# Second block's mixing loop: scores two heads ahead, output products inside the last turns, three weight remainders on GpSimd

## The chip, the cores and the metric

One core of one Trainium2 chip. The metric is device time in microseconds (us) of one execution. Below, PE is TensorE, DVE is VectorE, ACT is ScalarE, POOL is GpSimd and SP the engine whose queue issues the weight loads.

## What is computed

Two transformer blocks of two layers each on 256 tokens of width 1024, in float32. The change touches the mixing stage of the second block, once in each of its two layers:

```python
proj = h @ w_in[layer]
(qa, ka, va, qb, kb, vb, qi, ki, wi, qc, kc, vc) = jnp.split(proj, split_points, axis=-1)
...
oa = moba_attention(qa, ka, heads(va, N_HEADS_A))                    # 4 heads, softmax
ob = dsa_attention(qb, kb, heads(vb, N_HEADS_B), qi, ki, wi)         # 4 heads, top-64 keys, softmax
oc = stick_breaking_attention(heads(qc, N_HEADS_C), ...)             # 8 heads
...
o = jnp.concatenate([oa, ob, oc], axis=2)
o = (_rms(o).reshape(B, S, D_MIX) * out_g[layer]).astype(x.dtype)    # rms per head of 64
x = x + g2 * (o @ w_out[layer])
h = modulate(rmsnorm(x, norm_g[layer, 2]), sh3, sc3)
x = x + 0.5 * g3 * swiglu_2(h, ffn_w1[layer, 1], ffn_w3[layer, 1], ffn_w2[layer, 1])
```

Stick-breaking takes, with z the scaled scores, A = exp(z - sum over later keys of softplus(z)), where softplus(z) = max(z, 0) + log(1 + exp(-|z|)).

## The kernel before

**Weights.** All weights come as a stream of tiles of 128 x 2048 (1 MB) through a ring of four buffers (`stream_in`, L371): the load of tile p waits until PE has finished tile p - 4 (`tile_done`). Each product is made in three passes for precision (`triple`, L332): ACT rounds the tile to its high part (`high`, L320, semaphore `w_hi_ready`), DVE writes the remainder over the tile in the ring (`low`, L327, `w_lo_ready`), and PE multiplies high by high, high by low and low by high. The activations are split likewise into `h_hi` and `h_lo`.

**Tiles of the mixing stage.** Tile n is weight tile Z_QI + n. Tiles 0 to 14 project (`tile(n)`: 48 products of 256 columns each), 15 to 18 are the four tiles of `w_out` (named Z_O to Z_O + 3), and behind them the feed-forward begins (Z_O + 4 onward). ACT copies each projection out of PSUM (`evac(n)`, L2439 for n > 10) and then splits a tile three ahead. Tiles 13 and 14 share PSUM bank 3, so that tile 14 waits for `evac(13)`. While tiles 9 to 12 run, DVE selects the top 64 keys and makes remainders in between; the last, that of tile 14, ends just before the loop.

**The loop.** Eight turns handle one softmax head and one stick-breaking head each, and up to four more drain. The order of each engine is written out by hand; engines meet by semaphores only. On PE a head n needs `scores_sticks(n)` (L2307 to L2311), `flip(n)` (L2318: transposes of the probabilities), `sums(n)` (L2327 to L2331: the sum over later keys as products) and two `weigh` (L2347 to L2351: products with the values); for each pair of heads `turn_back` (L2360) transposes the normed output. DVE has `soften` (L2683: scale, mask; L2686, L2687: maxima), `stick` (L2692), `stick_log` (L2700: both inputs in SBUF), `stick_arg` (L2708), and for each pair `pair_stat` (L2713), `pair_scaled` (L535 to L537, L2725), `pair_low` (L2734). ACT has `exps` (L2481, L2483), `softplus` (L2492 to L2494), `flipped` (L2500: copies what flip wrote, `pt_ready`), `sticked` (L2504), and for each pair `pair_sq` (L2509), `pair_rstd` (L2514, L2515), `pair_high` (L2521). Heads n and n + 1 use different PSUM banks (4 and 5; 0 and 1 for the sticks), `sums` has bank 2, `flip` bank 6.

One turn of PE before the change:

```python
if i + 1 < HEADS_2: scores_sticks(i + 1)
if i in (0, 2): tile(13 + i // 2)
flip(i - 1); sums(i - 1)
if i >= 5 and i % 2 == 1: turn_back((i - 5) // 2)
weigh(n, 0, ...); weigh(n, 1, ...)      # n = i - 2
```

**Behind the loop.** `out_part(c, half, b, pair)` makes six products of 512 columns (two k, three passes) for token half b and column half c. 24 products per tile of `w_out`: first Z_O and Z_O + 1 for both token halves, turn_back 3 between them, then the other two tiles, with token half 0 first (`out_done`), token half 1 last. ACT splits Z_O + 3 and then Z_O + 4 (`next_high`), DVE makes their remainders; that of Z_O + 4 stands in `shift_dve` ahead of the gate (L724, L726: output times gate row), residual (L731), norm and shift. POOL, once the loop's last `weigh` is done, issues the loads of three rows of the modulation, 512 KB each as broadcast (L2802), and in the first layer that of `c_row` (L966).

## Time and profile before

| | us |
|---|---|
| median of 3 runs (lowest, highest) | 2841.31 (2838.57, 2844.32) |
| the profiled execution's own time | 2839.58 |
| its span, first to last instruction | 2837.5 |
| PE busy | 2766.8 (98%) |
| DVE busy | 1951.3 (69%) |
| ACT busy | 1366.8 (48%) |
| POOL busy | 228.7 (8%) |

The mixing loop runs twice: from about 2009 to 2060 and from about 2565 to 2618 us of the span. A busy PE is not one at its peak, since the ends of matmuls are modelled; start to start distances tell the pace. "Idle before" in a timeline row is the time in which the engine did nothing, and behind the arrow stands what ended it.

### The profile page before, as it was taken

To read this page: it belongs to the slowest core of one execution; us is meant where nothing else is said; L and a number is where in the kernel's file an instruction comes from. 1 tells how busy PE (TensorE), PEld (TensorE's weight loads), DVE (VectorE), ACT (ScalarE), POOL (GpSimd) and SP (SyncE) were. 2 spreads that over 40 slices of the span, in tenths; PEclk is the share of its full clock that TensorE was granted. 3 is DMA by queue.
4 is the path that set the end of the run, shared out by engine and by line. 5 is a ranking of instruction groups with operands and counts; after the bars stand their busy time and mean duration, and the time that the engine had idled before them with its cause. 6 is when DMAs were issued, how large, how long until landed. Compare 5 with 4: busy or idle time off the path is not lost.

```text
span 2837.5 us, 37822 instructions
## 1 busy us (share of the span) xinstructions
PE 2766.8 (98%) x16120; PEld 2426.8 (86%) x16120; DVE 1951.3 (69%) x2187; ACT 1366.8 (48%) x1562; POOL 228.7 (8%) x201
## 2 busy tenths in 40 slices
PE   8999999999999999999999999999899999999999
PEld 6889999998888889999998887878878878788787
DVE  6668876655666678877655667677876676677644
ACT  5444545455444445545454444444644444446433
POOL 0000420000000000520000000003000000030000
PEclk9999999999999999999999999999999999998999
DMA  8655433445766655333446666653266676442454
GB/s 306 257 220 183 149 125 136 164 164 210 263 261 248 248 208 189 138 136 132 171 165 228 257 255 243 260 218 134 90 244 251 239 274 253 177 150 95 176 189 148
DMA packets 82038, 564.42 MB, mean 199 GB/s; under 512 B 9072, under 2 KB 10576, under 8 KB 15952
## 3 DMA queue, kind: packets, MB, share of 16 engines
q1 hardware_dynamic: 66272, 465.47, 44.8%
q0 software_dynamic: 15600, 96.55, 9.0%
q8 instruction: 127, 2.08, 0.3%
q14 instruction: 39, 0.32, 0.0%
HBM read 560.86 MB, written 1.12 MB: 198 GB/s over the span
## 4 chain that ended last, share of the span: by engine, by line
PE 78%; DVE 13%; ACT 4%; POOL 2%; issue 2%; DMA 1%; SPq 0%; POOLq 0%; ACTq 0%; DVEq 0%
PE ps L332 71%; DVE ring_lo L327 4%; ACT w_hi L320 2%; POOL qk L2038 1%; PE ps L899 1%; POOL rope_a L2034 1%; DVE a_hg L1806 1%; DMA rows<-mod_rows 1%; DMA ring<-stream 1%; DVE e L1786 1%; DVE e L1785 1%; PE ps L1287 1%; DVE h_lo L576 0%; PE ps L1416 0%; PE ps L1442 0%
## 5 line engine op out<-in xcount | busy, mean ns | idle before, releaser
L327 DVE TENSOR_TENSOR ring_lo<-ring,w_hi 128x2048 fp32r<-128x2048 f32 x422 | 973.8, 2310 | 484.0 <-ACT w_hi L320 473.0
L320 ACT ACTIVATE w_hi<-ring 128x2048 fp32r<-128x2048 f32 x422 | 806.4, 1911 | 318.6 <-PE ps L332 188.0
L332 PE MATMUL ps<-w_hi,h_hi 128*128 128x512 f32 (+1 forms) x1920 | 728.9, 380 | 18.1 <-DVE ring_lo L327 9.0
L332 PE MATMUL ps<-w_hi,h_lo 128*128 128x512 f32 (+1 forms) x1920 | 717.0, 373 | 0.0
L332 PE MATMUL ps<-ring_lo,h_hi 128*128 128x512 f32 (+1 forms) x1920 | 716.3, 373 | 0.0
L332 PEld LDWEIGHTS ps<-w_hi,h_hi 128*128 128x128 f32 x1920 | 363.7, 189 | 85.6 <-DVE ring_lo L327 11.3
L332 PE MATMUL ps<-h_hi,w_hi 128*128 128x256 f32 x1488 | 431.6, 290 | 1.4 <-DVE h_lo L576 1.3
L332 PE MATMUL ps<-h_lo,w_hi 128*128 128x256 f32 x1488 | 423.0, 284 | 0.0
L332 PE MATMUL ps<-h_hi,ring_lo 128*128 128x256 f32 x1488 | 423.0, 284 | 0.0
L332 PEld LDWEIGHTS ps<-w_hi,h_lo 128*128 128x128 f32 x1920 | 363.2, 189 | 64.7
L332 PEld LDWEIGHTS ps<-ring_lo,h_hi 128*128 128x128 f32 x1920 | 363.8, 189 | 60.7 <-issue 1.0
L332 PEld LDWEIGHTS ps<-h_hi,w_hi 128*128 128x128 f32 x1488 | 287.6, 193 | 7.2 <-issue 5.9
L332 PEld LDWEIGHTS ps<-h_lo,w_hi 128*128 128x128 f32 x1488 | 287.8, 193 | 2.8 <-issue 2.4
L332 PEld LDWEIGHTS ps<-h_hi,ring_lo 128*128 128x128 f32 x1488 | 287.5, 193 | 0.0
L332 PE MATMUL ps<-w_hi,g_hi 128*128 128x512 f32 x576 | 224.6, 390 | 1.6 <-DVE g_lo L1083 1.6
L332 PE MATMUL ps<-w_hi,g_lo 128*128 128x512 f32 x576 | 224.1, 389 | 0.0
L332 PE MATMUL ps<-ring_lo,g_hi 128*128 128x512 f32 x576 | 224.1, 389 | 0.0
L993 DVE CUSTOM_DVE_ANT_0 e<-e,val 128x1024 f32<-128x1024 f32 x154 | 181.6, 1220 | 5.7 <-ACT val L1000 5.7
L1041 ACT ACTIVATE g_hi<-ps 128x512 fp32r<-128x512 f32 x80 | 47.7, 596 | 223.2 <-PE ps L899 223.2
L981 POOL DMA_DIRECT2D e<-ada x77 | 40.7, 529 | 1121.3 <-DVE mod_sum L993 822.9
L332 PEld LDWEIGHTS ps<-w_hi,g_hi 128*128 128x128 f32 x576 | 108.1, 188 | 24.7 <-DVE g_lo L1083 2.4
L332 PEld LDWEIGHTS ps<-w_hi,g_lo 128*128 128x128 f32 x576 | 108.1, 188 | 22.5
(359 smaller groups left out, 3437.4 us busy)
## 6 DMA issues: line engine op xcount, KB each, us to landing
ring<-stream SPq DMA_DIRECT2D x438, 1024.0 KB, 4.8
e<-ada POOLq DMA_DIRECT2D x77, 1024.0 KB, 6.2
rows<-mod_rows POOLq DMA_DIRECT2D x18, 512.0 KB, 5.7
rows<-gain_rows POOLq DMA_DIRECT2D x8, 512.0 KB, 4.8
val<-c_row POOLq DMA_DIRECT2D x4, 512.0 KB, 5.3
x<-x_in SPq DMA_DIRECT2D x4, 256.0 KB, 6.7
mem<-mem_t SPq DMA_DIRECT2D x1, 1024.0 KB, 16.2
out_t<-x SPq DMA_DIRECT2D x4, 256.0 KB, 2.1
```

What stands on the lines that cost most here:

```text
L320: nc.scalar.activation(hi_of(p), ring[:, p % RING, :], ACT.Copy).then_inc(S.w_hi_ready, 1)
L327: nc.vector.tensor_tensor(lo_of(p), ring[:, p % RING, :], hi_of(p).bitcast(F32), ALU.subtract).then_inc(S.w_lo_ready, 1)
L332: mm = nc.tensor.matmul(out, a, b, start=start and n == 0, stop=stop and n == 2, skip_group_check=group)
L899: mm = nc.tensor.transpose(ps[:, bank, a * T + b * P:a * T + (b + 1) * P], g_f[:, i % 2, b, a * P:(a + 1) * P], ident)
L981: pool.dma_start(e_buf[(i + 1) % 2][:].rearrange("p k t -> p (k t)"), ada[l * 2 * PER_FFN + first + i]).then_inc(ada_loaded[(i + done) % 2 ...
L993: ins = nc.vector.tensor_tensor_reduce(part, part, silu_c, 1.0, 0.0, ALU.mult, ALU.add, mod_sum[:, at + n:at + n + 1])
L1041: nc.scalar.activation(g_hi[:, g_slot(i - 1), :], ps[:, 2 * ((i - 1) % 2), :], ACT.Copy).then_inc(S.ghi_ready, 1)
L1287: mm = nc.tensor.matmul(ps[:, 4 + 2 * g + j // 2, at:at + n], sta[:, hd, t * P:(t + 1) * P], right, start=True, stop=True)
L1785: nc.vector.tensor_tensor(lo, lo, halves(hk, half)[0], ALU.mult)
L1786: nc.vector.tensor_tensor(hi_, hi_, halves(hq, half)[1], ALU.mult).then_inc(S.e_ready, 1)
L1806: ins = nc.vector.copy_predicated(dst.rearrange("p a (g two c) -> p a g two c", two=2, c=c)[:, :, :, 1, :], upper(mask, c).unsqueeze(1).br ...
L2034: nc.gpsimd.tensor_tensor(rope_a[:], part, cos1[:].unsqueeze(1).broadcast_to([P, 2, T]), ALU.mult).then_inc(S.pool_chain, 1)
```

## The change

On PE: tile 13 runs before the loop; scores 0 and 1 come ahead of it, tile 14 in turn 0, and each turn i then makes scores i + 2 between flip and sums (scores 4 at the end of turn 2). In turns 8 and 9 `out_ahead` puts the products of Z_O and Z_O + 1 for token half 0, 12 for each pair of heads; behind the loop token half 1 has 24 left, and turn_back 3 follows these. On ACT: `evac(13)` and `evac(14)` end turns 0 and 1, and the split of Z_O + 3 goes ahead of `pair_high` in the last turn. On DVE: the remainders of Z_O to Z_O + 2 are gone, `stick_log` comes before `stick_arg`, `pair_scaled` after both, and the remainder of Z_O + 3 ahead of the last `pair_low`. POOL makes the three remainders, four pieces of 128 x 512 each.

```diff
@@ -2285,7 +2285,7 @@
                                               fq[r, 4, 0:P * (qt + 1)], start=True, stop=True)
                         if i == len(even) - 1:
                             mm.then_inc(S.logit_done, 1)
-            for n in range(9, 13):
+            for n in range(9, 14):
                 tile(n)
 
             def scores_sticks(n):
@@ -2361,24 +2361,6 @@
                                                  o_tok[:, j, at:at + P], ident)
                 mm.then_inc(S.o_turned, 1)
 
-            scores_sticks(0)
-            for i in range(HEADS_2 + 2):
-                if i + 1 < HEADS_2:
-                    scores_sticks(i + 1)
-                if i in (0, 2):
-                    tile(13 + i // 2)
-                if 0 <= i - 1 < HEADS_2:
-                    flip(i - 1)
-                    sums(i - 1)
-                if i >= 5 and i % 2 == 1:
-                    turn_back((i - 5) // 2)
-                n = i - 2
-                if 0 <= n < HEADS_2:
-                    weigh(n, 0, n, pt2[:, n % 2, :], S.pt_ready, S.pv_done)
-                    weigh(n, 1, stick_head(n), st[:, 6 + n % 2, :], S.a_ready, S.o_done)
-            pe.wait_ge(S.arg_ready, nth(S.arg_ready, HEADS_2))
-            pe.wait_ge(S.scores_read, nth(S.scores_read, HEADS_2))
-
             def out_part(c, half, b, pair):
 
                 at = 2 * half + pair
@@ -2389,15 +2371,43 @@
                                 half == 1 and pair == 1 and i == 1)
                 return mm
 
-            pe.wait_ge(S.o_ready, nth(S.o_ready, 2))
+            def out_ahead(pair):
+
+                pe.wait_ge(S.o_ready, nth(S.o_ready, pair + 1))
+                if pair == 0:
+                    pe.wait_ge(S.zm_ready, nth(S.zm_ready, HEADS_2))
+                for c in range(2):
+                    pe.wait_ge(S.w_lo_ready, Z_O + c + 1)
+                    out_part(c, 0, 0, pair)
+
+            scores_sticks(0)
+            scores_sticks(1)
+            for i in range(HEADS_2 + 2):
+                n = i - 2
+                if i == 0:
+                    tile(14)
+                if 0 <= i - 1 < HEADS_2:
+                    flip(i - 1)
+                if i + 2 < HEADS_2 and i != 2:
+                    scores_sticks(i + 2)
+                if n >= HEADS_2 - 2:
+                    out_ahead(n - HEADS_2 + 2)
+                if 0 <= i - 1 < HEADS_2:
+                    sums(i - 1)
+                if 0 <= n < HEADS_2:
+                    weigh(n, 0, n, pt2[:, n % 2, :], S.pt_ready, S.pv_done)
+                if i >= 5 and i % 2 == 1:
+                    turn_back((i - 5) // 2)
+                if 0 <= n < HEADS_2:
+                    weigh(n, 1, stick_head(n), st[:, 6 + n % 2, :], S.a_ready, S.o_done)
+                if i == 2:
+                    scores_sticks(4)
+            pe.wait_ge(S.arg_ready, nth(S.arg_ready, HEADS_2))
             for c in range(2):
-                pe.wait_ge(S.w_lo_ready, Z_O + c + 1)
                 for pair in range(2):
-                    for b in range(2):
-                        mm = out_part(c, 0, b, pair)
+                    mm = out_part(c, 0, 1, pair)
                 mm.then_inc(S.tile_done, 1)
-                if c == 0:
-                    turn_back(3)
+            turn_back(3)
             pe.wait_ge(S.o_ready, nth(S.o_ready, 3))
             for c in range(2):
                 pe.wait_ge(S.w_lo_ready, Z_O + 2 + c + 1)
@@ -2524,27 +2534,24 @@
 
             nc.scalar.preload_act_table_set("natural_log_exp_and_others")
             for i in range(HEADS_2 + 4):
-                if 0 <= i - 2 < HEADS_2 and i != 3:
+                if 0 <= i - 2 < HEADS_2:
                     flipped(i - 2)
                 if i >= 5 and i % 2 == 1:
                     pair_rstd((i - 5) // 2)
                 if i < HEADS_2:
                     exps(i)
-                if i == 3:
-                    softplus(i)
-                    evac(14)
-                    flipped(i - 2)
                 if 0 <= i - 2 < HEADS_2:
                     sticked(i - 2)
+                if i == HEADS_2 + 3:
+                    next_high(act, Z_O)
                 if i >= 4 and i % 2 == 0:
                     pair_sq((i - 4) // 2)
                 if i >= 5 and i % 2 == 1:
                     pair_high((i - 5) // 2)
-                if i < HEADS_2 and i != 3:
+                if i < HEADS_2:
                     softplus(i)
-                if i == 1:
-                    evac(13)
-            next_high(act, Z_O)
+                if i < 2:
+                    evac(13 + i)
             next_high(act, Z_O + 1)
             shift_act(act, 2, Z_O + 2)
             ffn_act(act, FFN_D, 1, None, row=2 + DEPTH if l < DEPTH - 1 else None)
@@ -2743,20 +2750,17 @@
                 if i < HEADS_2:
                     soften(i)
                     stick(i)
-                if i == 3:
-                    low(dve, Z_V + 6 + HIGHS)
+                if 0 <= i - 1 < HEADS_2:
+                    stick_log(i - 1)
+                if 0 <= i - 2 < HEADS_2:
+                    stick_arg(i - 2)
                 if i >= 5 and i % 2 == 1:
                     pair_scaled((i - 5) // 2)
-                if 0 <= i - 2 < HEADS_2:
-                    stick_arg(i - 2)
-                if 0 <= i - 1 < HEADS_2:
-                    stick_log(i - 1)
-                if i == 1:
-                    low(dve, Z_V + 5 + HIGHS)
-                if i == 5:
-                    low(dve, Z_V + 7 + HIGHS)
                 if i >= 4 and i % 2 == 0:
                     pair_stat((i - 4) // 2)
+                if i == HEADS_2 + 3:
+                    dve.wait_ge(S.w_lo_ready, Z_O + HIGHS)
+                    low(dve, Z_O + HIGHS)
                 if i >= 5 and i % 2 == 1:
                     pair_low((i - 5) // 2)
 
@@ -2771,7 +2775,6 @@
                     dve.wait_ge(S.ada_done, nth(S.ada_done, PER_FFN))
                     vectors_two(chain, l + 1)
 
-            low(dve, Z_O + HIGHS)
             shift_dve(dve, chain, 2, Z_O + 2, row_count + 6, 0, z_ready)
             ffn_dve(dve, l, DEPTH, FFN_D, 1, False, products=l < DEPTH - 1, between=ahead)
             ready = ffn_ready(dve, FFN_D, 1)
@@ -2833,6 +2836,21 @@
                 nc.gpsimd.tensor_tensor(part, rope_a[0:r, 0:n, :], rope_b[0:r, 0:n, :],
                                         ALU.add).then_inc(S.rope_done, 1)
             send_mods(pool, l, 5, 9, sent + 2, sent + 2)
+            Z_O = tiles_2(l)[3]
+
+            def low_part(j, c):
+                p, at = Z_O + j, slice(c * 512, (c + 1) * 512)
+                if c == 0:
+                    pool.wait_ge(S.w_lo_ready, p)
+                    pool.wait_ge(S.w_hi_ready, p + 1)
+                ins = nc.gpsimd.tensor_tensor(lo_of(p)[:, at], ring[:, p % RING, at], hi_of(p)[:, at].bitcast(F32),
+                                              ALU.subtract)
+                if c == 3:
+                    ins.then_inc(S.w_lo_ready, 1)
+
+            for j in range(HIGHS):
+                for c in range(4):
+                    low_part(j, c)
             pool.wait_ge(S.o_done, nth(S.o_done, HEADS_2))
             row(ROW_GATE, l, 5)
             row(ROW_SHIFT, l, 6)
```

ACT at the loop's start, before: head 0's exponentials (L2481, L2483) and softplus (L2492 to L2494), those of head 1, and only then the copy of tile 13 (L2439) and the split of a weight tile (L320).

```order
L2481 ACTIVATE prob_20_66,e1<-prob_20_66,small 128x128
L2483 ACTIVATE prob_20_66,e1<-prob_20_66,small 128x256
L2492 ACTIVATE a_hg<-a_hg 128x384
L2493 ACTIVATE a_hg<-a_hg 128x384
L2494 ACTIVATE a_hg<-a_hg,one 128x384
L2481 ACTIVATE prob_21_67,e1<-prob_21_67,small 128x128
L2483 ACTIVATE prob_21_67,e1<-prob_21_67,small 128x256
L2492 ACTIVATE a_hg<-a_hg 128x384
L2493 ACTIVATE a_hg<-a_hg 128x384
L2494 ACTIVATE a_hg<-a_hg,one 128x384
L2439 ACTIVATE qk<-ps 128x512
L320 ACTIVATE w_hi<-ring 128x2048
```

The same place in the changed kernel, from head 0's second exponential on; its lines are 10 higher here (L2449 is the copy).

```order
L2493 ACTIVATE prob_20_66,e1<-prob_20_66,small 128x256
L2502 ACTIVATE a_hg<-a_hg 128x384
L2503 ACTIVATE a_hg<-a_hg 128x384
L2504 ACTIVATE a_hg<-a_hg,one 128x384
L2449 ACTIVATE qk<-ps 128x512
L320 ACTIVATE w_hi<-ring 128x2048
L2491 ACTIVATE prob_21_67,e1<-prob_21_67,small 128x128
L2493 ACTIVATE prob_21_67,e1<-prob_21_67,small 128x256
L2502 ACTIVATE a_hg<-a_hg 128x384
L2503 ACTIVATE a_hg<-a_hg 128x384
L2504 ACTIVATE a_hg<-a_hg,one 128x384
L2449 ACTIVATE qk<-ps 128x512
```

One copy and split stand after head 0 and one after head 1; before, tile 14's copy came in turn 3.

DVE behind the last pair, before: the refinement and scaling of pair 3 (L535 to L2725), its low part (L2734), and two remainders (Z_O + 3, Z_O + 4) ahead of the gate (L724).

```order
L537 SCALAR_TENSOR_TENSOR e<-e 128x8
L2725 TENSOR_TENSOR hk<-ps,e 128x512
L2734 SCALAR_TENSOR_TENSOR h_lo<-ps,v_now,h_hi 128x256 x2
L327 TENSOR_TENSOR ring_lo<-ring,w_hi 128x2048 x2
L724 TENSOR_TENSOR e<-ps,rows 128x512
L726 TENSOR_TENSOR e<-ps,rows 128x512
```

The same in the changed kernel (L2732 is the scaling, L2741 the low part).

```order
L537 SCALAR_TENSOR_TENSOR e<-e 128x8
L2732 TENSOR_TENSOR hk<-ps,e 128x512
L327 TENSOR_TENSOR ring_lo<-ring,w_hi 128x2048
L2741 SCALAR_TENSOR_TENSOR h_lo<-ps,v_now,h_hi 128x256 x2
L327 TENSOR_TENSOR ring_lo<-ring,w_hi 128x2048
L724 TENSOR_TENSOR e<-ps,rows 128x512
```

The remainder of Z_O + 3 has moved ahead of the low part; that of Z_O + 4 still stands between the low part and the gate.

## Rows read from the trace of the kernel before

**Rows 1.** The page, part 1: busy time and share of the span.

```profile
PE 2766.8 (98%) x16120; PEld 2426.8 (86%) x16120; DVE 1951.3 (69%) x2187; ACT 1366.8 (48%) x1562; POOL 228.7 (8%) x201
```

**Rows 2.** Timeline of PE: start us, us, engine, line, operation, idle before and releaser.

```profile
2009.04 0.34 PE L2307 MATMUL ps<-qk 64*128 64x128 f32 x1 [0.78 <-ACT qk L2439]
...
2019.69 0.38 PE L332 MATMUL ps<-h_hi,w_hi 128*128 128x256 f32 x1
...
2025.54 0.49 PE L2318 MATMUL ps<-con_sb,prob 128*128 128x128 f32 x3
...
2055.12 0.52 PE L2318 MATMUL ps<-con_sb,prob 128*128 128x128 f32 x3 [1.26 <-ACT prob_t L2500]
...
2058.74 0.66 PE L2360 MATMUL ps<-con_sb,hk 128*128 128x128 f32 x4 [0.93 <-DVE hk L2725]
...
2060.49 0.48 PE L332 MATMUL ps<-w_hi,h_hi 128*128 128x512 f32 x1
...
2575.39 0.38 PE L332 MATMUL ps<-h_hi,w_hi 128*128 128x256 f32 x1
```

**Rows 3.** Windows: stretch, its us, busy us of PE, PEld, DVE, ACT, POOL, clock.

```profile
2029.50:2054.50 25.00, 19.22 (x137) 16.66 (x137) 18.11 (x44) 17.52 (x48) 0.00 (x0) 0.93 0.02 6
```

**Rows 4.** Chain of waits in time, behind the first loop: start us, us, what.

```profile
2060.68 5.56 PE ps L332 x24
...
2066.25 6.76 DMA ring<-stream
...
2075.13 2.29 DVE ring_lo L327
2077.43 0.60 DVE e L724
```

**Rows 5.** DMA issues from 2626 to 2627: KB each, us to landing.

```profile
ring<-stream SPq DMA_DIRECT2D x1, 1024.0 KB, 4.7
```

**Rows 6.** Chain of waits behind the second loop.

```profile
2618.53 7.70 PE ps L332 x24
...
2637.62 0.70 DVE e L726
```

**Rows 7.** Timeline of DVE: the first softening.

```profile
2012.81 0.56 DVE L2683 SCALAR_TENSOR_TENSOR prob<-ps,con_sb 128x384 f32<-128x384 f32 x1
```

**Rows 8.** Timeline of ACT: exponentials of heads 0 and 1, copy of flip 6.

```profile
2014.05 0.40 ACT L2481 ACTIVATE prob<-prob,small 128x128 f32<-128x128 f32 x1 [2.05 <-DVE small L2687]
...
2016.56 0.39 ACT L2481 ACTIVATE prob<-prob,small 128x128 f32<-128x128 f32 x1
...
2054.51 0.47 ACT L2500 ACTIVATE prob_t<-ps 128x384 f32<-128x384 f32 x1
```

**Rows 9.** Timelines of POOL and of DVE in the rotary stage.

```profile
1957.48 1.28 POOL L2828 TENSOR_TENSOR rope_a<-qk,con_sb 128x512 f32<-128x512 f32 x1 [12.28 <-DVE qk L2608]
1959.45 3.20 POOL L2833 TENSOR_TENSOR qk<-rope_a,rope_b 128x512 f32<-128x512 f32 x1 [0.69 <-DVE rope_b L2617]
...
1979.73 3.26 POOL L2828 TENSOR_TENSOR rope_a<-qk,con_sb 128x512 f32<-128x512 f32 x1 [2.87 <-DVE qk L2608]
...
1959.23 2.28 DVE L327 TENSOR_TENSOR ring_lo<-ring,w_hi 128x2048 fp32r<-128x2048 f32 x1
1961.43 1.78 DVE L535 SCALAR_TENSOR_TENSOR e<-e 128x512 f32<-128x512 f32 x1
1963.24 0.69 DVE L536 TENSOR_TENSOR e<-e 128x512 f32<-128x512 f32 x1
...
1981.78 0.68 DVE L2617 TENSOR_TENSOR rope_b<-ps,con_sb 128x512 f32<-128x512 f32 x1
```

**Rows 10.** Windows around the norm ahead of the mixing stage.

```profile
1909.50:1913.00 3.50, 0.59 (x5) 0.35 (x3) 3.24 (x6) 1.93 (x5) 0.00 (x0) 1.00 0.94 384
...
1918.30:1923.27 4.97, 4.93 (x23) 4.96 (x24) 4.91 (x3) 1.31 (x2) 0.00 (x0) 0.50 0.02 3
```

**Rows 11.** Timeline of POOL: the row loads behind the first loop.

```profile
2061.23 1.57 POOL L2802 DMA_DIRECT2D rows<-mod_rows  x3 [74.12 <-PE ps L2351]
```

## The prediction

> **What bounds the kernel now.** I read first the page's share of each engine: PE is busy 98% of the span [rows 1], so a change pays only where PE waits, runs at half clock or is itself on the chain. Then the timeline of the mixing loop of the second block's first layer ("layer A"; the second, "layer B", runs the same 555.70 us later, by the starts of its tile 14 [rows 2]). There PE waits for ACT's copy of the transposed probabilities before flip 7 at 2055.12 and for DVE before turn_back 2 at 2058.74 [rows 2]. Third, the engines over the loop's middle: of 25.00 us PE is busy 19.22, DVE 18.11, ACT 17.52 [rows 3]. Nobody is full: the loop is a ring of waits through the three. Last, the chain behind the loop. In layer A it leaves PE after 24 output products (5.56 us) and goes through the load of the feed-forward's first weight tile (6.76), its split on ACT and its remainder on DVE (2.29); only then does DVE gate the first half row, at 2077.4 [rows 4]. In layer B, where that load takes 4.7 us [rows 5], the chain stays on PE's products, up to DVE's second gate product at 2637.62 [rows 6]. That one follows the first by 0.6 where nothing waits [rows 4], so B's gate counts as 2637.0, or 2081.3 on A's scale. This instant, the gate, sets the time of a layer.
>
> **Start of the loop.** Tile 13 now stands ahead of scores 0. Tile 12 ends at 2008.26 (scores 0 at 2009.04 after 0.78 of idle [rows 2]); a tile takes 5.85 (2019.69 to 2025.54 [rows 2]), so scores 0 starts near 2014.05. A head's scores take 0.9 there, so DVE's first softening starts at 2014.95, where it was 2012.81 [rows 7]: 2.1 us later. ACT begins 1.24 after a softening (2012.81 to 2014.05) and takes 2.51 for a head's exponentials and softplus (2014.05 to 2016.56 [rows 8]), so to 2018.7. Only then comes the copy of tile 13 (0.6), for which tile 14 waits, as both lie in PSUM bank 3. PE stands from about 2015.8 to 2019.3; tile 14 runs to 2025.2, against 2025.54. ACT copies tile 14 and splits the next weight tile (1.9) and is free at 2027.6. Before, it got there at 2029.5, 1.9 later, but with two more heads' exponentials and softplus (5.0), one copy (0.47 [rows 8]) and one stick exponential (0.5) done: 6.1 us of work more.
>
> **Middle of the loop.** From there to the copy that frees flip 7 (2054.51 [rows 8]) ACT did 17.5 us of work and waited 7.5 [rows 3]. Now it has 17.5 + 6.1 to do. Its waits shrink, since scores come two turns ahead, but they don't go: `pair_high` stands ahead of softplus in each odd turn and still needs the scaling on DVE and turn_back on PE. Following the queues turn by turn with these durations, I get two such waits of about 2 us and small ones, 4.6 in all. 2027.6 + 23.6 + 4.6 = 2055.8, so flip 7 starts at 2056.5, after 0.5 for the copy and a restart: 1.4 later than before. The three remainders that leave DVE's loop (2.29 each) earn nothing by this: DVE has 7 us to spare in the stretch [rows 3], and at 2038 the remainder lay beside turn_back and `pair_high`.
>
> **Tail of the loop.** From flip 7 to the first output product took 5.37 us (2055.12 to 2060.49 [rows 2]), some 1.2 of it the stand before turn_back 2 (0.93 as idle, the rest its restart); 4.15 of work stay. Two groups of 12 products go in, at 5.56/24 = 0.232 each, 5.6. PE leaves the loop at T = 2056.5 + 9.7 = 2066.2. Before, it left at 2060.49 and had those 24 products yet to do: 2066.05. So the filling alone gains nothing: the largest stand of the last turns is before flip 7, and the first group is queued behind it.
>
> **GpSimd's remainders.** One 128x512 product takes it 1.28 us alone and 3.20 beside a DVE remainder; the DVE instruction behind took 1.78 where the next took 0.69; a DVE product of PSUM and one SBUF operand beside a busy GpSimd took 0.68, no more [rows 9]. So in the loop only `stick_log`, with both inputs in SBUF, can be hit. The twelve products end near 2033 (the third tile starts when ACT is done, at 2027.6), or at 12 x 3.26 = 39 us after 2012.8, 2052, at worst, before their first use at 2056.9: no wait of PE. But stick_log 1 and 2 fall at 2027.7 and 2030.9, and ACT waits for what follows them. Bounds 0 and 2.6 (two whole products); by the row's excess, 1.78 - 0.69 = 1.09 each, 2.2; I take 1.5, as they need not meet exactly. The Trainium skill (SBUF — State Buffer, Who interferes with whom) says that a DVE instruction with two SBUF inputs and a GpSimd one that reads SBUF lock each other out for the whole instruction; by that rule, with which the row agrees, the term would be up to 2.6.
>
> **Clock.** In the trace 3.5 us with 0.59 of PE work were followed by the half clock, 1.2 GHz, with 23 products in 4.93 us, 0.214 each [rows 10]. The new stand before tile 14 is as long. At half clock its 48 products, 5.85/48 = 0.122 each, cost up to 48 x 0.092 = 4.4 more; nothing if the clock holds. I take 1.5: only the products until the clock is back count. T = 2069.2.
>
> **After the loop.** The load on layer A's chain starts with the last product of the first output tile. That was 5.76 after T (2066.25 less 2060.49); of 24 products 12 remain, so it is now T + 2.95. The row loads on GpSimd's queue are issued 0.75 after T (2061.23 [rows 11]); the weight load came 5.0 after them and will come 2.2 after. It competes with them from its start. Least, 6.76 as before; most, a landing 11.8 after the row loads' issue as before (2061.23 to 2073.01), T + 12.5, if only the bytes count. I take T + 10.7. From landing to gate are 4.4 (2073.0 to 2077.4): T + 15.1 = 2084.3, against 2077.4, **6.9 later**. Layer B has one row load fewer: landing T + 10, gate T + 14.4 = 2083.6, against 2081.3, **2.3 later**. What is behind the gate (norm, transposes, feed-forward) moves as a whole. 9.2 in all.
>
> **Sum.** The profiled execution took 2839.58 (span 2837.5); plus 9.2 is 2848.8. The median of the runs is 2841.31; by it, 2850.5. I put 2849.5. With the open terms at their lower ends (no lock-out, clock held, load 6.76 in A and 4.7 in B) A is 2.9 later and B 3.1 earlier: 2839.4. At the upper (2.6, 4.4, landings T + 12.5 and T + 11.2) A is 12.7 later, B 7.5: 2859.8.
>
> **Rivals.** *No change* (0.25): the lower ends hold, 2839.4 to 2843. For it: two of the terms can be nothing. Against: the load's place next to the row loads is no chance. *Faster* (0.17), by filling: if scores two turns ahead bring flip 7 to 2050.8 instead of 2056.5, T is the 2060.5 of before with 24 products done. Then the gate is at T + 14.1 in A (2.8 earlier) and T + 12.05 in B (8.8 earlier, its half clock, 7.70 for 24 products [rows 6] where A has 5.56, gone): 2828. It gains over 0.2% from T = 2063.4 down. For it: ACT and DVE have 7 us of waits there. Against: ACT's late start, and pair_high's place in its queue. *Half clock behind the loop in both layers* (0.12): in B it cost 2.1 on 24 products and as much in the loop; 4.3 a layer on top of the forecast, 2858. *GpSimd late* (0.03): it would need over 43 us; each us beyond is one us in each layer, some 2855. My forecast has the rest, 0.43.
>
> **Numbers.** 0.2% is 5.7 us, about what a measurement of this kernel can tell. Slower by more: forecast, half clock and GpSimd, 0.58. Within: 0.25. Faster: 0.17. The range runs from 2832, part of the way into the faster case, to 2860.
>
> **What would show it.** In the changed kernel's layer A: PE idle some 3.5 us before tile 14, ended by ACT's copy; flip 7 between 2056 and 2060 with an output product right after it; turn_back 2 behind the second group with no wait; GpSimd's products 1.3 to 3.3 us each and done before 2050; one or two stick_logs of over 0.55 us; the feed-forward's first tile issued 3 us after the loop, its remainder on DVE ending after the products that the gate needs. If flip 7 comes before 2051, or the load lands within 5 us, I am wrong on the side of faster.

## The result, and the profile after

| | before | after |
|---|---|---|
| median us (lowest to highest) | 2841.28 (2838.57 to 2844.32) | 2863.98 (2862.16 to 2864.03) |
| the profiled execution | 2839.58 | 2864.03 |
| mean granted clock of PE | 0.992 | 0.983 |

The changed kernel takes 1.0082 of the time of the kernel before (95% interval 1.0066 to 1.0098), 22.7 us more. Slower was forecast, at 2849.5 us; the measured time lies outside the range of 2832 to 2860.

I compared the start of each matmul with the same matmul in the trace before. The changed kernel is already 5.0 us late at 1982 us, in code that is the same in both. It loses 11.9 us in layer A and 7.3 in layer B, 19.2 together. Of the 5.0, 2.5 and 1.1 come up at two stretches of the first block that went at 1.2 GHz here and at 2.4 GHz before, as the windows of the two traces show (stretch, its us, busy us and instructions of PE, PEld, DVE, ACT, POOL, clock, DMA share, GB/s). Kernel after:

```profile
385.60:392.40 6.80, 6.80 (x34) 6.80 (x34) 6.80 (x4) 1.91 (x1) 4.37 (x3) 0.50 0.13 54
1218.50:1225.30 6.80, 6.80 (x33) 6.80 (x33) 5.76 (x3) 5.90 (x8) 6.58 (x3) 0.50 0.05 19
```

Kernel before:

```profile
385.60:392.40 6.80, 6.80 (x60) 6.80 (x58) 6.80 (x4) 1.96 (x2) 3.80 (x2) 1.00 0.04 17
1218.50:1225.30 6.80, 6.80 (x59) 6.80 (x58) 5.12 (x3) 5.91 (x8) 3.98 (x2) 1.00 0.29 93
```

Such stretches come and go between executions: a second trace of the kernel before (first experiment) has one at 1230.8 to 1237.6, with PE as busy. So "own scale" below means a time less what the trace was late at the last product of tile 12, ahead of the loop (5.0 us for the changed kernel in layer A, 17.2 in B).

**Layer A on PE**, the timeline's rows that answer to [rows 2] (start us, us, operation, idle before and its releaser):

```profile
2018.95 0.37 PE L2307 MATMUL ps<-qk 64*128 64x128 f32 x1
...
2024.37 0.58 PE L332 MATMUL ps<-h_hi,w_hi 128*128 128x256 f32 x1 [3.83 <-ACT qk L2449]
...
2052.55 0.52 PE L2318 MATMUL ps<-con_sb,prob 128*128 128x128 f32 x3 [2.39 <-ACT prob_t L2510]
...
2065.60 0.88 PE L2318 MATMUL ps<-con_sb,prob 128*128 128x128 f32 x3 [1.84 <-ACT prob_t L2510]
2066.13 0.78 PE L332 MATMUL ps<-w_hi,h_hi 128*128 128x512 f32 x1
...
2076.62 0.48 PE L332 MATMUL ps<-w_hi,h_hi 128*128 128x512 f32 x1
```

Scores 0 comes at 2014.0 on its own scale and tile 14 at 2019.4, behind the stand foretold (2014.05, 2019.3). Flip 7 comes at 2060.6, where 2056.5 was forecast before the terms for the clock and GpSimd, and the first output product behind the loop, T, at 2071.6 (forecast 2069.2).

**Layer A on ACT**, whose queue decides this (rows that answer to [rows 8], and its four largest waits):

```profile
2021.23 0.40 ACT L2491 ACTIVATE prob<-prob,small 128x128 f32<-128x128 f32 x1 [4.22 <-DVE small L2694]
...
2023.74 0.58 ACT L2449 ACTIVATE qk<-ps 128x512 f32<-128x512 f32 x1
...
2031.75 0.60 ACT L2449 ACTIVATE qk<-ps 128x512 f32<-128x512 f32 x1 [3.14 <-PE ps L332]
...
2049.57 0.84 ACT L2531 ACTIVATE h_hi<-ps,v_now 128x256 fp32r<-128x256 f32 x2 [1.98 <-PE ps L2360]
...
2062.63 0.84 ACT L2531 ACTIVATE h_hi<-ps,v_now 128x256 fp32r<-128x256 f32 x2 [3.70 <-PE ps L2360]
```

ACT stands 4.22 us (for the last 2.3 of them tile 13 lies ready in PSUM, as PE goes on to scores 0 at 2018.95), does head 0, copies tile 13 at 2023.74, does head 1, and then stands 3.14 us for tile 14, which could not start before that copy.

**The clock in layer A** (windows, columns as above; [rows 10] are the ones of before):

```profile
2024.00:2027.41 3.41, 3.04 (x14) 3.04 (x15) 0.42 (x1) 3.40 (x7) 1.15 (x1) 0.50 0.00 0
2054.72:2068.37 13.65, 11.70 (x49) 10.55 (x48) 7.32 (x20) 8.11 (x22) 0.00 (x0) 0.50 0.00 0
2099.10:2105.90 6.80, 5.90 (x19) 4.36 (x17) 6.77 (x9) 4.21 (x7) 0.00 (x0) 0.50 0.00 0
```

PE ran at 1.2 GHz for 3.41 us from the start of tile 14, for 13.65 us over turns 7 and 8, and for 6.80 us behind the gate.

**Behind the loop** the chain of waits (start us, us, what), which answers to [rows 4], and the DMA issues from 2075 to 2082 us:

```profile
2076.81 2.82 PE ps L332 x12
...
2079.65 8.85 DMA ring<-stream
2088.60 1.93 ACT w_hi L320
...
2090.62 2.29 DVE ring_lo L327
2092.91 0.60 DVE e L724
```

```profile
rows<-mod_rows POOLq DMA_DIRECT2D x3, 512.0 KB, 5.2
ring<-stream SPq DMA_DIRECT2D x1, 1024.0 KB, 8.8
val<-c_row POOLq DMA_DIRECT2D x1, 512.0 KB, 10.5
```

The weight load goes out 3.03 us after T and takes 8.85 us where it took 6.76 [rows 4]. The gate (L724) comes 16.2 us after T, at 2087.8 on its own scale.

### The profile page after: what moved, and what is told of

The parts are those of the page before. It is cut to its first block, busy times and chain, and to the rows that moved or that the text cites. A ratio compares the mean times of both kernels' runs of the same rounds, so it can differ in the third digit from the quotient of the medians.

```text
span 2862.1 us, 37846 instructions
## 1 busy us (share of the span) xinstructions
PE 2782.5 (97%) x16120; PEld 2442.3 (85%) x16120; DVE 1940.2 (68%) x2181; ACT 1366.5 (48%) x1562; POOL 260.1 (9%) x225
## 4 chain that ended last, share of the span: by engine, by line
PE 84%; DVE 8%; ACT 3%; DMA 2%; POOL 2%; issue 1%; SPq 0%; POOLq 0%; ACTq 0%; DVEq 0%
PE ps L332 75%; DVE ring_lo L327 3%; ACT w_hi L320 2%; PE ps L899 1%; POOL qk L2038 1%; DMA ring<-stream 1%; PE ps L1287 1%; POOL rope_a L2034 1%; DMA rows<-mod_rows 1%; PE ps L530 1%; PE ps L1416 0%; PE ps L1442 0%; DVE e L993 0%; DVE e L1786 0%; DVE e L1785 0%
## 5 line engine op out<-in xcount | busy, mean ns | idle before, releaser
L327 DVE TENSOR_TENSOR ring_lo<-ring,w_hi 128x2048 fp32r<-128x2048 f32 x416 | 960.5, 2311 | 491.1 <-ACT w_hi L320 479.5
L320 ACT ACTIVATE w_hi<-ring 128x2048 fp32r<-128x2048 f32 x422 | 806.4, 1911 | 323.5 <-PE ps L332 185.9
```

The costliest lines, as they stand in the source:

```text
L320: nc.scalar.activation(hi_of(p), ring[:, p % RING, :], ACT.Copy).then_inc(S.w_hi_ready, 1)
L327: nc.vector.tensor_tensor(lo_of(p), ring[:, p % RING, :], hi_of(p).bitcast(F32), ALU.subtract).then_inc(S.w_lo_ready, 1)
```

## The experiments

Theory A: the loss has two separate parts, tile 13 ahead of scores 0, and the products in turns 8 and 9 with the load that they bring into the row loads; GpSimd's part is about free. The rivals blame GpSimd, the new order of the turns, or the clock alone. Every ratio is against runs of the kernel before on the same chip. The experiments ran on several chips, where the median of the kernel before lies between 2838.8 and 2841.3 us, so a difference in us between two changed kernels is good to some 2 us.

**1. The kernel before once more**, with no edit, to see what differs between executions.

> The kernel before, unchanged, under a second name. Theory A (the 4 us that the changed kernel lost before the first layer of the second block, at two half-clock stretches in the first block, are an accident of where the clock falls, not of the change): executions of the same code differ by up to 6 us, and the granted clock differs between executions from 0.992 to about 0.985. Rival (the code of the change shifts the first block by itself): this kernel stays at 2841 +- 3 in every execution with clock 0.992 in all.

2839.14 us, ratio 0.9998 (0.9988 to 1.0007). Its trace is 7.4 us later than the first one at the end: 2.7 in the first block, 0.5 at the norm ahead of the second, 4.0 around the end of loop A, where PE went at 1.2 GHz from 2053.4 to 2070.5. One profile of this kernel can lie that far from another.

**2. GpSimd's remainders alone.** In the kernel before, the three `low` calls of DVE's loop are taken out and GpSimd's twelve products put in ahead of its row loads.

```
-                if i == 1:
-                    low(dve, Z_V + 5 + HIGHS)
...
+            for j in range(HIGHS):
+                for c in range(4):
+                    low_part(j, c)
```

> Before, with the three remainders of Z_O to Z_O + 2 on GpSimd as the only change. Theory A (order costs, GpSimd does not): within 3 us of before, since the DVE remainders in the loop lay beside other work and one stick_log is late by 0.4 us. Rival B (the lock-out between GpSimd and DVE is a main cost): 4 us or more above before, with several DVE instructions of two SBUF inputs over 1.2 us in the loop.

2843.1 us, ratio 1.0007 (0.9997 to 1.0017): no difference clear of noise, and at most 0.17%. A group of four takes some 5 us beside DVE here, and one `stick_log` a layer takes 1.62 us instead of 0.55 beside such a group:

```profile
2020.34 1.62 DVE L2700 SCALAR_TENSOR_TENSOR a_hg<-a_hg 128x384 f32<-128x384 f32 x1 [0.65 <-ACT a_hg L2494]
```

In the changed kernel, too, one `stick_log` of the eight in layer A is stretched. The changed kernel's rows on POOL and DVE:

```profile
2034.29 5.60 POOL L2846 TENSOR_TENSOR ring_lo<-ring,w_hi 128x512 fp32r<-128x512 f32 x4 [3.00 <-ACT w_hi L320]
```

```profile
2037.78 0.97 DVE L2707 SCALAR_TENSOR_TENSOR a_hg<-hb,a_hg 128x384 f32<-128x384 f32 x1 [0.63 <-ACT a_hg L2504]
```

0.97 instead of 0.55 us, once: of the 1.5 us of the forecast 0.4 are seen.

**3. The changed kernel without the products in turns 8 and 9**; all 24 stand behind the loop again.

```
-                if n >= HEADS_2 - 2:
-                    out_ahead(n - HEADS_2 + 2)
...
-                for pair in range(2):
-                    mm = out_part(c, 0, 1, pair)
+                for pair in range(2):
+                    for b in range(2):
+                        mm = out_part(c, 0, b, pair)
```

> The changed kernel without output products in turns 8 and 9: all 24 of Z_O and the 24 of Z_O + 1 behind the loop, as before. Theory A (the products gain nothing in the turns and bring the feed-forward tile's load into the row loads): 4 to 8 us faster than the changed kernel (2856 to 2860), the load from 6 to 7 us again in the first layer. Rival C (the products do fill waits): 5 to 10 us slower than the changed kernel.

2853.5 us, ratio 1.0050 (1.0035 to 1.0065): 10.5 us less than the changed kernel, more than expected. The load of the feed-forward's first tile, issued 5.3 us behind the first row load, takes 5.96 us in layer A and is no longer on the chain, and flip 7 is late all the same (2060.1 on its own scale, against 2060.6): the products had little part in that.

**4. Tile 13 back behind scores 0 and 1**, the rest as changed.

```
-            for n in range(9, 14):
+            for n in range(9, 13):
...
             scores_sticks(1)
+            tile(13)
```

> The changed kernel with tile 13 behind scores 0 and 1 instead of ahead of them, everything else as changed. Theory A (the stand of PE before tile 14 and the half clock behind it cost the start): tile 14 starts at 2017 to 2018 on the time scale of before instead of 2019.5, no half clock there; 5 to 9 us faster than the changed kernel over both layers. Rival D (the loop is bound by ACT, whatever the start): within 2 us of the changed kernel.

2851.78 us, ratio 1.0040 (1.0025 to 1.0055): 12.2 us less, again more than expected. Tile 14 waits 0.69 us, no half clock follows it, and flip 7 comes at 2056.6 on its own scale, 4.0 earlier.

**5. Both taken back.** Scores two steps ahead and GpSimd's remainders are what is left of the change.

> The changed kernel without the products in turns 8 and 9 and with tile 13 back behind the first two scores; left of the change are scores two steps ahead and the remainders on GpSimd. Theory A (the two parts hurt apart from each other: the products in the last turns cost 10.5 us by the run without them, tile 13 ahead of scores 0 costs 12.2 us by the run with it back; the rest of the loop's new order is about free): 2839 to 2844 us, the kernel before within 0.2%. Theory B (both cost through the same thing, the last turns at half the clock, so undoing the second gives little more): 2848 to 2853 us. Theory C (scores two steps ahead cost something by themselves): 2846 us or more with tile 14 on its old place and the turns of the loop later than before by more than 1 us in layer A.

2841.24 us, ratio 1.0013 (1.0004 to 1.0022), some 3.7 us over its neighbours of 2838.82. The two parts add up: 10.5 and 12.2 are 22.7, closer than the noise allows. By the traces, layers A and B together lose 19.2 us in the changed kernel, 11.9 in number 3, 11.0 in number 4 and 1.4 here. Theory A holds, with at most a few us for the rest.

**6. The products in the last turns, in the kernel before**, and nothing else.

```
+                if n >= HEADS_2 - 2:
+                    out_ahead(n - HEADS_2 + 2)
                 if 0 <= i - 1 < HEADS_2:
                     sums(i - 1)
```

> The kernel before with the products of the o half in turns 8 and 9, and nothing else of the change. Theory A (the products stand ahead of sums and turn_back in turns that decide when the last head is done, and bring the w half and the load of the weight tile into the row loads): 2844 to 2850 us, with the tile's load over 7.5 us as in the changed kernel (8.85 us) and the first output product behind the loop no earlier than before. Theory B (without tile 13 in front the products fill waits of the last turns, and 12 of 24 products less stand behind the loop): 2832 to 2838 us, the first gate product of layer A 2 to 5 us earlier. If neither part costs alone but both together, it is within 0.2% of 2841 us.

2848.69 us, ratio 1.0032 (1.0020 to 1.0045): about 9 us by themselves, whatever stands at the loop's head (6.1 of them in the two layers by its trace, 5.1 in A). The products do fill a little: PE leaves the loop at 2064.9 on its own scale with 24 of them done, where it had done as many at 2066.05 before. The load takes back more than that. Its chain behind loop A has the same load:

```profile
2068.59 2.84 PE ps L332 x12
...
2071.44 8.85 DMA ring<-stream
```

So the 8.85 us belong to the place, 2.3 us behind the first row load (2.5 in the changed kernel, 5.0 before), and "they fill waits" falls as a gain.

**7. The row loads behind the weight load**: GpSimd also waits for the second output tile.

```
             pool.wait_ge(S.o_done, nth(S.o_done, HEADS_2))
+            pool.wait_ge(S.tile_done, Z_O + 1)
```

> The changed kernel, but GpSimd's five row loads behind the loop wait until the second output tile is done, so that the load of the weight tile goes out ahead of them or with them. Theory A (the 8.85 us of the weight load in layer A are the row loads sharing the DMA queues with it): the load takes 5 to 6.8 us, the first gate product is 2 to 3.5 us earlier in layer A and 1 to 3 in layer B, 2858 to 2861 us. Theory B (the load's time is its own or that of other traffic): it stays at 8 us or more, 2863 to 2865 us. Theory C (the rows now arrive too late for gate and norm): 2865 us or more, with a wait on the rows ahead of the first gate product.

2866.99 us, ratio 1.0091 (1.0077 to 1.0106), no better than the changed kernel. The weight load is indeed early (ACT waits 1.14 us for it, not 4.94), but now the rows are late; the chain of waits:

```profile
2080.69 10.17 DMA rows<-mod_rows
...
2090.88 2.29 DVE ring_lo L327
2093.17 0.60 DVE e L724
```

The gate is at 2088.9 on its own scale, against 2087.8. It needs the rows and the tile, and the loads together take as long in either order: from the first issue to the last landing of the rows, `c_row` and the next two weight tiles, 4 MB, 13.3 us here and 13.8 in the changed kernel. Part of the late gate is DVE's own order: `shift_dve` waits for the rows ahead of the remainder of Z_O + 4 (L327), though ACT had split that tile by 2086.2. With the remainder ahead of that wait the gate could be some 2.2 us earlier, an estimate from the rows above; no run tried it. The change let them start together, where the kernel before had the rows nearly landed. The rows can't be fetched sooner, since their buffer lies over `a_hg`, the loop's own scratch.

**8. Work of no use in the waits of the kernel before.** 22 products 128x128 into a free PSUM bank in turns 7 to 9: 9 behind flip 6, 9 ahead of flip 7, 4 ahead of turn_back 2.

```
+                    if i == 8:
+                        pe.wait_ge(S.zm_ready, nth(S.zm_ready, HEADS_2 - 1))
+                        busy(9)
                     flip(i - 1)
+                    if i == 7:
+                        pe.wait_ge(S.zm_ready, nth(S.zm_ready, HEADS_2 - 1))
+                        busy(9)
```

> The kernel before with 22 products 128x128 of no use on TensorE in turns 7 to 9 of the second block's loop, in places where it waited, so that it has something to do there. Theory A (the half clock in the last turns and behind the loop comes from TensorE standing between its heads' products, and it costs time there): the stretch at half clock around and behind the loop (2053.4 to 2070.5 us in the second run of the kernel before) is gone or shorter than 7 us in both layers, and the time is 2833 to 2839 us. Theory B (the clock falls for other reasons, or the products cost as much as the clock gives back): the stretch stays and 2841 to 2846 us.

2833.25 us, ratio 0.9978 (0.9970 to 0.9987), faster than the kernel before by some 6 us. The windows around loop B's end, kernel before and then this one:

```profile
2605.90:2623.00 17.10, 16.54 (x67) 15.24 (x66) 7.47 (x21) 6.95 (x17) 1.57 (x3) 0.50 0.15 46
```

```profile
2605.00:2623.00 18.00, 18.00 (x120) 16.25 (x119) 9.01 (x24) 9.44 (x20) 1.58 (x3) 1.00 0.37 135
```

Seventeen us at 1.2 GHz are gone. The trace gains 5.5 us in B and 1.3 in A, where the first trace had the half clock for 3.4 us only. Note that PE was 97% busy in the stretch before: busy time is long because products are slow, and a busy share doesn't tell a full engine from a slow one.

**9. The same kind of products in the changed kernel**: 15 ahead of tile 14, 13 around flip 6, 8 ahead of flip 7.

```
                 if i == 0:
+                    busy(15, 6)
                     tile(14)
+                if i == 7:
+                    pe.wait_ge(S.zm_ready, nth(S.zm_ready, HEADS_2 - 1))
+                    busy(9)
+                if i == 8:
+                    busy(8)
                 if 0 <= i - 1 < HEADS_2:
                     flip(i - 1)
+                if i == 7:
+                    busy(4)
```

> The changed kernel with 36 products 128x128 of no use on TensorE: 15 ahead of tile 14, 13 around flip 6, 8 ahead of flip 7, all where it stood. Theory A (a large part of what the change costs is the clock: it stood at half in 2024.0 to 2027.4 and 2054.7 to 2068.4 in layer A, and in both layers ahead of the first output product): these stretches are gone, the first output product behind the loop of layer A is 3 to 6 us earlier, and the time is 2853 to 2859 us. The rest of the loss, the load of 8.85 us and tile 14 behind its eviction, stays. Theory B (the clock is a consequence and costs little where the last heads wait for VectorE and ScalarE): 2861 to 2865 us. Theory C (the products are in the way: their time is added): over 2866 us.

2860.28 us, ratio 1.0072 (1.0060 to 1.0085). At tile 14 it worked: full clock, and from scores 0 ACT is done with its copy and split 1.3 us earlier in A and 2.2 in B. In turns 6 and 7 it missed. PE's stand is ahead of flip 5, and the clock had fallen at 2047.8 before the first of the others, of which nine then ran at half speed in flip 6's way:

```profile
2053.79:2057.94 4.15, 4.15 (x20) 4.15 (x21) 1.21 (x5) 0.52 (x1) 0.00 (x0) 0.50 0.00 0
```

From scores 0, flip 7 comes 1.8 us later than in the changed kernel, so the turns lost 3.1. But from 2058.0 on the clock was full, and that prices the tail: from flip 7 to T the same 61 records of PE take 9.72 us here and 11.02 in the changed kernel. Number 9's window, then the changed kernel's:

```profile
2064.23:2073.95 9.72, 9.72 (x61) 8.67 (x62) 3.11 (x10) 2.72 (x8) 0.00 (x0) 1.00 0.00 0
```

```profile
2065.60:2076.62 11.02, 11.02 (x61) 9.71 (x62) 3.11 (x10) 2.72 (x8) 0.00 (x0) 0.87 0.01 1
```

**10. The same, a turn earlier**: 11 ahead of flip 5, in the PSUM bank of the running sums, so behind a wait for DVE.

```
+                if i >= 6 and i <= 8:
+                    pe.wait_ge(S.arg_ready, nth(S.arg_ready, i - 1))
+                    busy({6: 11, 7: 2, 8: 9}[i], 2)
                 if 0 <= i - 1 < HEADS_2:
                     flip(i - 1)
+                if i == 6:
+                    busy(3, 2)
```

> The changed kernel with products of no use again, put where the run before showed TensorE standing: 15 ahead of tile 14, 11 ahead of flip 5 and 3 behind it, 2 ahead of flip 6, 9 ahead of flip 7. In the run before, TensorE stood 2.39 us ahead of flip 5 and the clock fell at 2047.8, ahead of the first of the 21 others, which then went at half clock in the way of flip 6. Theory A (the clock is a large part of the loss in layer A): no half clock from 2018 to the first output product, which comes 3 to 6 us earlier than in the changed kernel measured from scores 0, and the time is 2853 to 2858 us. Theory B (the half clock lies over waits for ScalarE and VectorE and costs little): half clock gone, but the first output product less than 2 us earlier, 2859 to 2864 us. If the half clock stays in the loop, neither is tested.

2868.77 us, ratio 1.0099 (1.0082 to 1.0116). The added wait spoilt it; PE's row ahead of flip 5:

```profile
2050.84 0.58 PE L2385 MATMUL ps<-con_sb 128*128 128x128 f32 x1 [3.72 <-DVE a_hg L2726]
```

PE stood 3.72 us for a bank instead of 2.39 for flip 5, and then had the 11 to do. The half clock stayed, for 6.8 and 3.4 us, so this says nothing of the theories. With scores two steps ahead I found no bank that is free at this point. What the half clock costs in the changed kernel's turns 6 and 7 was therefore not measured in that kernel. But number 5 has the same order there, and in its layer B the clock was full over this part. ACT's `pair_high` behind flip 6, which waits for PE's turn_back, and the window from flip 6 to it, in number 5's layer B:

```profile
2608.51 0.84 ACT L2535 ACTIVATE h_hi<-ps,v_now 128x256 fp32r<-128x256 f32 x2 [1.80 <-PE ps L2360]
```

```profile
2605.63:2608.51 2.88, 2.71 (x24) 2.45 (x23) 1.62 (x6) 0.75 (x3) 0.00 (x0) 1.00 0.00 0
```

The same window in layer A of the changed kernel, whose wait is 3.70:

```profile
2057.56:2062.63 5.07, 4.96 (x22) 4.40 (x23) 1.91 (x6) 1.04 (x5) 0.00 (x0) 0.50 0.00 0
```

So the half clock is worth 1.9 us of that wait. In the order of the kernel before it shows as well: the wait is 1.58 us in both layers of number 8, 2.76 and 2.13 in the kernel before.

**11. Products in the norm's waits as well**, on top of number 8: 24 ahead of the second block's projection.

```
             for q in (2 * b, 2 * b + 1):
+                if fill and q >= 1:
+                    for _ in range((0, 15, 3, 3)[q]):
+                        nc.tensor.matmul(ps[:, 0, 0:P], ident, ident, start=True, stop=True, ...)
```

> The kernel before with the 22 products of no use in the last turns of the loop, as in the run with 2833.2 us, and 24 more in the waits of the norm ahead of the second block's projection (1910.1 to 1918.3 us in the kernel before), whose half clock (1913.0 to 1923.3) reaches 5 us into the projection. Theory A (work in a wait holds the clock there too): the half clock at 1913 and 2469 is gone, both projections start at full clock, 2 to 3 us less in each, 2826 to 2830 us. Theory B (the norm's waits are too long for it or the projection is bound by something else there, weights or VectorE): 2832 to 2836 us.

2832.91 us, ratio 0.9977 (0.9966 to 0.9988). The clock did what theory A expected, the time is in theory B's range. The window of the norm and that of the projection's first 6.7 us:

```profile
1914.03:1922.28 8.25, 7.30 (x64) 6.92 (x63) 7.75 (x15) 5.61 (x11) 0.00 (x0) 1.00 0.50 201
1922.28:1929.00 6.72, 6.72 (x59) 6.72 (x58) 5.53 (x6) 2.18 (x4) 0.00 (x0) 1.00 0.00 0
```

59 products where the kernel before had 37 in 6.70 us. The stage is 2.5 us shorter in A and 2.3 in B than in number 8's trace. Yet the median is that of number 8. In this trace 3.4 us more than in number 8's were lost in the first block, and 1.2 GHz from 2596.9 to 2603.7 took back 2.5 (ACT's wait before `pair_high` is 4.08 us there, 1.58 in number 8); whether that is chance or a price of holding the clock elsewhere stays open.

**12. ScalarE copies tile 13 at once.** The changed kernel with one call moved on ACT, ahead of head 0's exponentials.

```
+            evac(13)
             for i in range(HEADS_2 + 4):
...
-                if i < 2:
-                    evac(13 + i)
+                if i == 1:
+                    evac(14)
```

> The changed kernel, but ScalarE copies tile 13 out of PSUM at once, in front of head 0's exponentials, where it stood 4.22 us for VectorE. Theory A (tile 13 in front costs through the chain tile 13's copy behind head 0, tile 14, its copy ahead of the next heads' work on ScalarE): TensorE's stand of 3.83 us before tile 14 is under 0.8, no half clock at tile 14, ScalarE's wait of 3.14 for tile 14 is under 0.5, flip 7 is 4 to 5 us earlier measured from scores 0, 4 to 6 us less in each layer, 2852 to 2857 us. Theory B (the heads start 4 to 5 us late and ScalarE is full from there, so that the later start is the price): tile 14 is early, but flip 7 less than 1.5 us earlier and 2860 to 2864 us.

2850.22 us, ratio 1.0030 (1.0018 to 1.0041): 13.8 us less than the changed kernel (12 to 15, by the medians of the kernel before beside them or by the ratios). Rows of PE (tile 14, flip 7) and of ACT (copies of tiles 13 and 14):

```profile
2017.22 0.39 PE L332 MATMUL ps<-h_hi,w_hi 128*128 128x256 f32 x1
...
2057.39 0.52 PE L2318 MATMUL ps<-con_sb,prob 128*128 128x128 f32 x3 [2.17 <-ACT prob_t L2510]
```

```profile
2015.82 0.60 ACT L2449 ACTIVATE qk<-ps 128x512 f32<-128x512 f32 x1 [2.06 <-PE ps L332]
...
2023.28 0.60 ACT L2449 ACTIVATE qk<-ps 128x512 f32<-128x512 f32 x1
```

This trace is 3.24 us earlier than the changed kernel's at scores 0. So tile 14 comes 3.9 us earlier against that, its copy 5.2 and flip 7 5.0; ACT's wait for the tile is gone. Tile 13 stands ahead of scores 0 here too. Not the place of the tile was dear, but the wait for its copy.

**13. The same without the products in turns 8 and 9**, that is the edits of numbers 3 and 12 together:

```
-                if n >= HEADS_2 - 2:
-                    out_ahead(n - HEADS_2 + 2)
...
+            evac(13)
```

> The same, without the products in turns 8 and 9. If the two parts of the loss add as before (10.5 us for the products), theory A gives 2841 to 2846 us, within 0.2% of the kernel before, and theory B 2850 to 2853 us.

2841.56 us, ratio 1.0006 (0.9997 to 1.0014): of the 22.7 us at most 4 are left by the interval, and it holds zero. Theory A's two parts, both named, account for the loss.

## Why the prediction was wrong

It had the right sign, the stand before tile 14 and the load among the row loads, and 9.2 us where the two layers lost 19.2: 11.9 in A for 6.9, 7.3 in B for 2.3. The other 3.5 us of the median are within its interval (18.8 to 27.8). In the profiled run 3.6 us arose at the first block's two stretches; how much of the median is chance of that kind is not shown.

The step that failed is the term for the clock. I let the clock fall at tile 14 alone, for 1.5 us, and gave the last turns, the tail and the feed-forward's start nothing. In layer A the runs price it at 1.3 us at tile 14 (number 9), 1.9 in ACT's wait behind flip 6 (number 5 against the changed kernel) and 1.3 between flip 7 and T (number 9), 4.5 up to T, and behind the gate the loss grows by another 1.4 over 6.8 us at 1.2 GHz, which no run prices apart.

- **Start of the loop.** Scores 0, the stand and tile 14's start were right within 0.1 us (2008.26 and 5.85 make 2014.11, not 2014.05, and the terms of the 6.1 us of work more make 6.0; neither matters). Tile 14 ended at 2026.6 on its own scale, not 2025.2, since its first half went at 1.2 GHz. ACT was done with its copy and the next split at 2029.1, not 2027.6. Number 12 gives 5.0 us at flip 7 for the stand, the half clock behind it and ACT's wait for tile 14 together.
- **Middle of the loop.** I wrote that ACT would wait 4.6 us from there to flip 7, two waits of about 2 us and small ones. The work of 23.6 us was right, but it waited 7.2: 1.98 and 3.70 before `pair_high`, and five before the stick exponentials of 1.5 together. At full clock the second was 1.80 (number 5), so the queues were followed rightly and the clock was left out. In number 12, without the stand, ACT waits 7.5 us in the same stretch: this excess has nothing to do with tile 13. With the 1.5 of the step ahead, flip 7 came 5.5 us later than before, where I had 1.4 and some 3 more for lock-out and clock.
- **GpSimd.** 1.5 us forecast, 0.4 seen, no difference in number 2. The Trainium skill (SBUF — State Buffer, Who interferes with whom) has a DVE instruction with two inputs in SBUF contend with a GpSimd one that reads SBUF; the stretched `stick_log`s, 0.97 us here and 1.62 in number 2 for 0.55, are such instructions, and the traces agree so far. One of the eight in layer A met a product, and the worst case of 2.6 us did not come. That the term was too large made up for part of the missing clock, and this was luck.
- **Tail.** 9.7 us from flip 7 to T forecast, 11.0 measured, 9.7 at full clock (number 9).
- **The load.** Issued at T + 3.03 (forecast 2.95), landed at T + 11.9 (forecast 10.7), near the upper bound, "if only the bytes count": number 7 agrees with that bound. It made the gate 1.1 later.
- **Behind the gate.** The loss grows from 10.5 at the feed-forward's first product (at 2101.46, in the trace before at 2085.97; less 5.0) to 12.6 within the stretch at 1.2 GHz that ends at 2105.9, and is 11.9 at 2118, as the kernel before waits for a remainder in between. Together in A: 2.4 at T, 1.1 at the load, 1.4 here, 4.9 of the 5.0 missed.
- **Layer B.** The gate came 14.6 us after T (14.4 forecast). T was 3.9 us late, with twice as long a half clock at tile 14 (6.8 us, 2.2 by number 9), 7.5 us of ACT's waits in the middle and a tail of 11.3, and 0.9 was lost behind the gate.
- **Rivals.** The rival with half clock in both layers, 2858, was nearest, but I had tied it to the loop's end and gave it 0.12. *Faster by filling* fell with number 6: the products stand in turns whose end sets the layer, and pull the load into the row loads. *GpSimd late* fell with number 2, and its last product ends at 2034.9 on its own scale, 26 us before the first use of such a remainder.

## What to carry to other kernels

When work is moved ahead of a loop, follow its result too: another engine must copy it out before the next tile can go. Number 12 got back more than half of the loss by letting ScalarE make that copy in the time it stood idle, with the tile still ahead of the loop. Work moved forward to fill waits also moves the transfers that its end releases; ask what these will meet. And where TensorE stands repeatedly for one or two us, look at the granted clock: products of no use in these waits made this kernel 0.22% faster in number 8. In numbers 9 and 10 they came behind the fall of the clock or behind an added wait, and cost time in these turns.

## What the runs showed of the hardware

- The clock fell without one long stand. Ahead of the 13.65 us at 1.2 GHz in layer A, PE had stood 2.39 us before flip 5 and 0.91 behind it, with work between. It then stayed at 1.2 GHz in stretches in which PE was 86% (11.70 of 13.65 us) and, in the kernel before, 97% (16.54 of 17.10) busy by the profile.
- The same code differs between executions: stretches of 6.8 us at 1.2 GHz in the first block, where PE was 100% busy, cost 1.1 to 2.5 us each and were in some traces and not in others; the half clock around the end of loop A of the kernel before was 3.4 us long in one trace and 17.1 in another. This makes some 5 us of difference between two profiles mean little until the clock is compared.
- The same 61 records of PE between flip 7 and T took 9.72 us at 2.4 GHz and 11.02 at a mean clock of 0.87, and PE counted as 100% busy in both.
- Loads under way together took as long in either order, 13.8 and 13.3 us for the same 4 MB: a weight tile of 1024 KB took 8.85 us beside the row loads and 4.7 where it came later behind them [rows 5], and put first it made the rows take 10.17.
